# Gather and weight rings of a decoder layer: v ring 6 to 5 slots, query weight ring 4 to 5 and 6

## What is computed

```python
def peer_layer(x, w_q, sub_keys, u_table, v_table):
    q = (tok @ w_q).reshape(T, PEER_HEADS, 2, KEY_DIM)
    s = jnp.einsum('thcd,hckd->thck', q, sub_keys)
    s1, i1 = lax.top_k(s[:, :, 0], PEER_TOPK)
    s2, i2 = lax.top_k(s[:, :, 1], PEER_TOPK)
    cand = (s1[..., :, None] + s2[..., None, :]).reshape(T, PEER_HEADS, PEER_TOPK * PEER_TOPK)
    top, pos = lax.top_k(cand, PEER_TOPK)
    ...
    idx = e1 * N_KEYS + e2
    gates = jax.nn.softmax(top, axis=-1)
    ...
        u = u_table[ic]
        act = jax.nn.gelu(jnp.einsum('cd,chkd->chk', xc, u), approximate=False) * gc
        v = v_table[ic]
        return jnp.einsum('chk,chkd->cd', act, v)
```

## Time and profile before

| | |
|---|---|
| median of three runs | 3369.57 us (3368.59 to 3376.63) |
| profiled execution, its own time | 3396.82 us |
| its span | 3395.0 us |
| TensorE, matmuls | 2514.1 us busy, 74% of the span |
| VectorE | 2129.6 us, 63% |
| GpSimd | 2080.4 us, 61% |
| ScalarE | 859.2 us, 25% |
| DMA | 1209.32 MB, mean 356 GB/s |
| gathers of u and v | 1024 each, 1073.87 MB |
| granted clock of TensorE, mean | 0.843 |

### The profile page before, as it was taken

How to read it: one execution, slowest core, us unless ns; L and a number is a source line. 1 busy time by engine, 2 the same in 40 slices (tenths; PEclk the granted TensorE clock), 3 DMA queues, 4 the chain that set the end, 5 groups by cost and what they waited for, 6 DMA issues and landing times.

```text
span 3395.0 us, 33094 instructions
## 1 busy us (share of the span) xinstructions
PE 2514.1 (74%) x10304; PEld 1258.0 (37%) x10304; DVE 2129.6 (63%) x5664; ACT 859.2 (25%) x2635; POOL 2080.4 (61%) x2164
## 2 busy tenths in 40 slices
PE   8967888868888677767766677667976698765555
PEld 6754445534455233323333233322433243331111
DVE  2585556854669555884659646694658847586442
ACT  5334533125331132112211122112321133111111
POOL 0377566775667665665666656665666656666665
PEclk8989899988999787877898788887888878887777
DMA  9599899998999999998999989998899989999998
GB/s 306 175 338 379 324 363 398 399 373 304 363 394 377 398 374 341 406 380 305 345 379 397 365 301 344 395 393 329 322 371 405 377 294 331 383 405 350 381 369 318
DMA packets 383118, 1209.32 MB, mean 356 GB/s; under 512 B 43488, under 2 KB 84448, under 8 KB 382944
## 3 DMA queue, kind: packets, MB, share of 16 engines
q0 software_dynamic: 294912, 1073.87, 83.5%
q1 hardware_dynamic: 83616, 132.94, 11.0%
q10 hardware_dynamic: 4416, 0.40, 0.1%
HBM read 1199.20 MB, written 7.86 MB: 356 GB/s over the span
## 4 chain that ended last, share of the span: by engine, by line
PE 41%; issue 18%; DVE 12%; POOL 10%; DMA 7%; another core or an unknown queue 7%; ACT 4%; SPq 0%; DVEq 0%; ACTq 0%; POOLq 0%
PE psum L1014 19%; PE psum L843 5%; DVE big L1534 5%; POOL big L750 5%; POOL big L761 5%; DMA big<-in_peer_v,big 4%; PE psum L887 4%; PE psum L979 3%; PE psum L921 3%; PE psum L946 3%; DMA big<-in_peer_u,big 2%; PE psum L903 1%; DVE big L1347 1%; ACT big L1160 1%
## 5 line engine op out<-in xcount | busy, mean ns | idle before, releaser
L1014 PE MATMUL psum<-big 128*64 128x512 f32 x4096 | 1256.2, 743 | 550.7 <-issue 544.0
L761 POOL DMA_INDIRECT big<-in_peer_v,big x1024 | 1009.2, 986 | 718.1 <-PE psum L1014 311.8
L750 POOL DMA_INDIRECT big<-in_peer_u,big x1024 | 1025.8, 1002 | 443.8 <-issue 292.4
L1534 DVE CUSTOM_DVE_ANT_0 big<-big,psum 128x1024 f32<-128x1024 f32 x714 | 859.4, 1218 | 355.2 <-DMA big<-in_peer_u,big 283.1
L1014 PEld LDWEIGHTS psum<-big 128*64 128x64 f32 x4096 | 317.3, 161 | 1214.5 <-issue 1198.6
L1160 ACT ACTIVATE big<-big 128x64 f32<-128x64 f32 x1024 | 294.7, 339 | 863.5 <-PE psum L1014 400.9
L1534 DVE CUSTOM_DVE_ANT_0 big<-big 128x1024 f32<-128x1024 f32 x310 | 374.7, 1224 | 77.5 <-DMA big<-in_peer_u,big 72.2
L1347 DVE CUSTOM_DVE_ANT_0 big<-psum,big 128x512 f32<-128x512 f32 (+3 forms) x192 | 110.7, 577 | 425.4 <-PE psum L887 218.1
L979 PEld LDWEIGHTS psum<-big 128*128 128x128 f32 x2048 | 253.3, 201 | 94.1 <-issue 82.7
L979 PE MATMUL psum<-big 128*128 128x128 f32 x2048 | 272.4, 289 | 16.7 <-ACT big L1228 9.6
L887 PE MATMUL psum<-KT,big 64*128 64x512 f32 (+3 forms) x384 | 202.2, 613 | 79.6 <-issue 47.8
(11 more groups left out here) (141 smaller groups left out, 2137.2 us busy)
## 6 DMA issues: line engine op xcount, KB each, us to landing
big<-in_w_peer_q SPq DMA_DIRECT2D x108, 512.0 KB
big<-in_w_in SPq DMA_DIRECT2D x24, 1024.0 KB, 12.4
big<-in_peer_u,big POOLq DMA_INDIRECT x1024
big<-in_peer_v,big POOLq DMA_INDIRECT x1024
big<-in_w_out SPq DMA_DIRECT2D x2, 4096.0 KB, 22.7
big<-in_w_out SPq DMA_DIRECT2D x16, 512.0 KB
big<-in_w_in SPq DMA_DIRECT2D x28, 256.0 KB
V<-in_w_in SPq DMA_DIRECT2D x20, 256.0 KB
```

What stands on the lines that cost most here:

```text
L750: nc.gpsimd.indirect_dma_start(out=u_row(g), out_offset=None, in_=peer_u, in_offset=bass.IndirectOffsetOnAxis(ap=idx[:, t % 2, u_pick(p):u ...
L761: nc.gpsimd.indirect_dma_start(out=v_ring[:, g % RV, :], out_offset=None, in_=peer_v, in_offset=bass.IndirectOffsetOnAxis(ap=idx_v[:, t % ...
L1014: last = nc.tensor.matmul(pAcc[half_rows(c), n, :], sel[:, (g + c) % RD, :], v_ring[:, (g + c) % RV, n * COLS:(n + 1) * COLS], start=False ...
L1534: v.tensor_tensor_reduce(out=row_, in0=row_, in1=hn_ps if g >= MOVE_PICK else hn[:, hn_buf(t), :], scale=1.0, scalar=0.0, op0=ALU.mult, op ...
```

## The change

The v ring gets five slots instead of six, and the u ring keeps five to the end. The weight ring gets five, and from tile 3 on a sixth, in the half of `hn` that was the u ring's sixth. All 16 chunks of a tile are now used in reverse order in every other tile from tile 3 on (before, the four blocks were reversed and the four parts of a block stood in one order), so that the last five or six chunks of a tile can be the first of the next. Tile 3 keeps 5 chunks and tiles 4 to 7 keep 6, where 4 were kept. The slots are now given out by a list (`list_places`) that names for each load the one that it replaces.

```diff
-RU, RV = 5, 6
-WIDER_FROM = 61 * RU
-RW = 4
+RU, RV = 5, 5
+RW = 5
+WIDER_FROM = NARROW
...
+def query_part(t, n):
+
+    return divmod(4 * (PH // 2) - 1 - n if t >= EARLY and (t - EARLY) % 2 == 0 else n, 4)
...
+def ring_of(t):
+    return RW + 1 if t >= WIDER_FROM else RW
...
-    return t >= EARLY and i < RW
+    return t >= EARLY and i < ring_of(t - 1)
...
-                load_of[t, i] = load_of[t - 1, w_chunks(t - 1) - RW + i]
+                load_of[t, i] = load_of[t - 1, w_chunks(t - 1) - 1 - i]
...
+def list_places():
+
+    free, slot, before, widened = list(range(RW)), [], [], False
+    held = []
+    for m, (t, i) in enumerate(W_LOADS):
+        prev = None
+        if t >= WIDER_FROM and not widened:
+            widened, r = True, RW
+        elif free:
+            r = free.pop(0)
+        else:
+            prev = min(held, key=lambda o: W_ENDS[o])
+            held.remove(prev)
+            r = slot[prev]
+        slot.append(r)
+        before.append(prev)
+        held.append(m)
+    return slot, before
...
-                if m >= RW:
-                    te, ie = W_ENDS[m - RW]
+                if W_BEFORE[m] is not None:
+                    te, ie = W_ENDS[W_BEFORE[m]]
                     sp.wait_ge(w_used, w_first(te) + ie + 1)
+                elif m == W_WIDER:
+                    sp.wait_ge(y_stored.sem, y_stored.at(1, 1))
...
-                if u_before(g) is not None:
-                    pool.wait_ge(u_used.sem, u_before(g) + 1)
-                elif g >= RU:
-                    pool.wait_ge(y_stored.sem, y_stored.at(1, 1))
+                if g >= RU:
+                    pool.wait_ge(u_used.sem, g - RU + 1)
...
-                        last = nc.tensor.matmul(pT[:, j % 2, i * P:(i + 1) * P], w_ring[:, m % RW, k, i * P:(i + 1) * P],
-                                                turned[:, 2 * kp + k, :], start=(kp == 0 and i == 0 and k == 0),
+                        last = nc.tensor.matmul(pT[:, j % 2, i * P:(i + 1) * P], w[:, k, i * P:(i + 1) * P],
+                                                turned[:, 2 * part_ + k, :], start=(kp == 0 and i == 0 and k == 0),
```

More of the change, by code:

```diff
@@ L205, in w_place @@
     return lin(t, slot_of(t, 27 + 6 * (i // 4) + i % 4))
+def query_part(t, n):
+    return divmod(4 * (PH // 2) - 1 - n if t >= EARLY and (t - EARLY) % 2 == 0 else n, 4)
 def query_block(t, j):
-    return PH // 2 - 1 - j if t >= EARLY and (t - EARLY) % 2 == 0 else j
+    return query_part(t, 4 * j)[0]
+def ring_of(t):
+    return RW + 1 if t >= WIDER_FROM else RW
 def kept(t, i):
-    return t >= EARLY and i < RW
+    return t >= EARLY and i < ring_of(t - 1)
 def list_chunks():
@@ L233 @@
 W_LOADS, W_ENDS, W_LOAD_OF = list_chunks()
[L236 to L250, removed]
+def list_places():
[15 more added lines that the diff above has]
+    return slot, before
+W_SLOT, W_BEFORE = list_places()
+W_TURN = [W_SLOT[:m].count(r) for m, r in enumerate(W_SLOT)]
+W_WIDER = W_SLOT.index(RW)
 def hn_buf(t):
@@ L360, in hybrid_layer, with w_slot @@
         rms_x = w_out_flat[:, 8080:8088]
-        def u_row(g):
-            return hn[:, 1, :] if u_slot(g) == RU else u_ring[:, u_slot(g), :]
+        def w_slot(m):
+            return hn[:, 1, :] if W_SLOT[m] == RW else w_flat[:, W_SLOT[m]]
         key_raw = V[:, 3:5, :].rearrange("p t n -> p (t n)").rearrange("p (g n) -> p g n", g=2 * PH)
@@ L454, in hybrid_layer @@
         y_stored = signal("y_stored", 1, 16)
-        w_loaded = [sem(f"w_loaded{r}") for r in range(RW)]
-        u_loaded = [sem(f"u_loaded{r}") for r in range(RU + 1)]
+        w_loaded = [sem(f"w_loaded{r}") for r in range(RW + 1)]
+        u_loaded = [sem(f"u_loaded{r}") for r in range(RU)]
         v_loaded = [sem(f"v_loaded{r}") for r in range(RV)]
@@ L625, in load_w @@
                 t, i = W_LOADS[m]
-                if m >= RW:
-                    te, ie = W_ENDS[m - RW]
+                if W_BEFORE[m] is not None:
+                    te, ie = W_ENDS[W_BEFORE[m]]
                     sp.wait_ge(w_used, w_first(te) + ie + 1)
+                elif m == W_WIDER:
+                    sp.wait_ge(y_stored.sem, y_stored.at(1, 1))
                 if i < w_out_chunks(t):
-                    sp.dma_start(w_flat[:, m % RW], w_out[i * P:(i + 1) * P, :]).then_inc(w_loaded[m % RW], 16)
+                    sp.dma_start(w_slot(m), w_out[i * P:(i + 1) * P, :]).then_inc(w_loaded[W_SLOT[m]], 16)
                 else:
[L632 to L635, removed]
+                    block, kp = query_part(t, i - w_out_chunks(t))
+                    sp.dma_start(w_slot(m).rearrange("p (k n) -> p k n", k=2),
+                                 w_peer_q[2 * kp * P:2 * (kp + 1) * P, block * COLS:(block + 1) * COLS]
+                                 .rearrange("(k p) n -> p k n", p=P)).then_inc(w_loaded[W_SLOT[m]], 16)
             def store_q(u):
@@ L724, in _ @@
                     for m in range(RW, len(W_LOADS)):
-                        if w_place(*W_ENDS[m - RW]) == lin(e, s):
+                        place = lin(2, SLOTS - 4) if m == W_WIDER else w_place(*W_ENDS[W_BEFORE[m]])
+                        if place == lin(e, s):
                             load_w(m)
@@ L745, in gather_u @@
                     pool.wait_ge(idx_ready.sem, idx_ready.at(t, p // TOPK + 1))
-                if u_before(g) is not None:
-                    pool.wait_ge(u_used.sem, u_before(g) + 1)
-                elif g >= RU:
-                    pool.wait_ge(y_stored.sem, y_stored.at(1, 1))
+                if g >= RU:
+                    pool.wait_ge(u_used.sem, g - RU + 1)
                 nc.gpsimd.indirect_dma_start(
-                    out=u_row(g), out_offset=None, in_=peer_u,
+                    out=u_ring[:, g % RU, :], out_offset=None, in_=peer_u,
                     in_offset=bass.IndirectOffsetOnAxis(ap=idx[:, t % 2, u_pick(p):u_pick(p) + 1], axis=0))\
-                    .then_inc(u_loaded[u_slot(g)], 16)
+                    .then_inc(u_loaded[g % RU], 16)
             def gather_v(g):
@@ L942, in out_proj @@
                 if w_out_chunks(t):
-                    pe.wait_ge(w_loaded[m % RW], 16 * (m // RW + 1))
-                w = w_flat[:, m % RW] if w_out_chunks(t) else w_out_sb[:, k, :] if t else w_out_rows[:, k, :]
+                    pe.wait_ge(w_loaded[W_SLOT[m]], 16 * (W_TURN[m] + 1))
+                w = w_slot(m) if w_out_chunks(t) else w_out_sb[:, k, :] if t else w_out_rows[:, k, :]
                 for n in range(2):
@@ L1527, in dot_row @@
                 g = t * PICKS + p
-                dve.wait_ge(u_loaded[u_slot(g)], 16 * (u_turn(g) + 1))
+                dve.wait_ge(u_loaded[g % RU], 16 * (g // RU + 1))
                 if g == MOVE_PICK or p == 0 and t > IN_PSUM:
```

6 lines of the change are left out of this document (3 added, 3 removed).

## The result

| | us |
|---|---|
| before, median of 4 runs | 3370.76 (3368.59 to 3376.63) |
| after, median of 4 runs | 3411.39 (3401.69 to 3424.10) |
| ratio | 1.0098, 95% interval 1.0064 to 1.0131 |
| profiled execution of after: time, span | 3401.83, 3400.0 |

The change makes the kernel slower by 33 us by the ratio (22 to 44 by its interval), 41 by the medians.

The account below looks back on a forecast made before the run. No compute engine was full; the DMA engines were nearly so outside attention, and late gathers, held most by v slots, lost time. Terms -12 + 0 + 0 + 8 + 15 + 35 + 8 = +54 on 3369.6 gave 3424 us, range 3360 to 3500.

Parts of the forecast that it names:

- Fewer loads: Query stretches: 9 weight transfers of 512 KB go, 12 us gained, bounds 0 and 15.
- Weights deeper ahead: Query matmuls: they never wait for a weight transfer, so the fifth and sixth weight slots gain nothing more, 0 us.
- u ring back to five: From pick 305 on: no gain of the sixth u slot is seen in attention, so 0 us, bound 20.
- v ring: All v gathers: with five slots every second one needs its slot a whole pair later; +8, +15, +35 and +8 by stretches.
- Tail: Last 12 v pairs after the last u gather: a loop of two pairs, 4.0 us a pair, +8 us (6 to 16).
- Last stage: Gathers, dots and row sums only: some seven late releases plus the low clock, +15 us, bounds 0 and 27.
- Paced stretches: Between attention and query stretches: a third of the last stage's rate, +35 us, bounds 0 and 99.
- attention: Attention stretches: half a microsecond in some of about 30 bursts of pairs, +8 us, bounds 0 and 40.
- Query stretches: Where query weights load beside gathers: DMA engines stay full with fewer gathers queued, 0 us; below 400 GB/s, forecast too low.
- Bytes alone: Rival, whole kernel: five slots keep the DMA as full as six, only saved bytes count, 3356 us; chance 0.15.
- Even: Rival: the tail's 8 us and the bytes' 12 nearly cancel, -4 to +8, 3366 to 3378 us; chance 0.20.
- The v ring everywhere: Rival, every stretch: the odd gather's wait lengthens each pair, +100 to +190, 3470 to 3560 us; chance 0.15.

Follow-up runs that it names:

- its repetition: The changed kernel run once more, on one chip with its parts, against the kernel before: 3410.95 us, ratio 1.0090.
- experiment 2: The kernel before with the u ring at five slots to the end, v ring six, weights as before: 3379.16 us, ratio 0.9993.
- experiment 5: The kernel before with the last 24 v picks also using the five empty u slots, eleven in all: 3372.50 us, ratio 0.9980.
- experiment 8: The kernel before with u ring five, 4 weight loads fewer, and the last 24 v picks in eleven slots, on a faster chip: 3148.63 us, ratio 0.9982.
- experiment 1: The kernel before with only the v ring cut from six slots to five, all weight loads kept: 3419.68 us, ratio 1.0131.
- experiment 3: The changed kernel with v ring six and weight ring four, then five from tile 3; 4 loads fewer than before: 3370.12 us, ratio 0.9969.

## Why the prediction was right, point by point

Forecast +54 us, 3424; measured 3411, +33 by the ratio, and +30 and +41 in two other sets. The case that the forecast took (+10 to +100, the v ring outweighing the bytes) is the one that came. That the total lies so near is in part luck, as the points below tell: one term was ten times too large, and another was worked out from it.

By stretches, measured between the starts of fixed pairs of v rows (512 pairs, 0 to 511; of each 64 the query stretch is 43 to 60, attention 11 to 26, paced what lies between, in the table from pair 0 to 448; last stage 448 to 499, tail 499 to 511): (a) mean of after and its repetition, less the mean of before and of experiments 2 and 5; (b) the change on the faster chip less experiment 8 on such a chip, which has 4 of the 9 loads off and the longer ring in the tail.

| stretch | forecast | (a) | (b) |
|---|---|---|---|
| paced and attention | +35 +8 | +27 | +39 |
| query, with the 9 loads | -12 | -8 | -8 |
| last stage | +15 | +2 | +2 |
| tail | +8 | +7 | +14 |
| sum | +54 | +28 | +47 |

For the tail, (a) leaves experiment 5 out. Paced stretches and attention stand together since profiles of the same rings trade time between them: beside the rows of tiles 2 to 6 attention takes 489 to 519 us in the three with six v slots, and the paced stretches 931 to 962. Their sum is 1451 to 1460, and with five slots 1454 (experiment 1), 1467 and 1485. From pair 0 to 448 single profiles of the same rings lie up to 19 us apart, so the +27 and +39 are rough, and one profile with five slots stands inside the range of six.

- *Fewer loads, -12.* Right. 99 loads, 4.72 MB less. The query stretches beside the rows of tiles 2 to 6, which are the fronts of tiles 3 to 7 with the nine loads, take 508 to 509 us in the three profiles with loads taken away (after, its repetition, experiment 3) and 514 to 521 in the four without: 9.5 us less by the means, and 9 to 14 by the runs. What one load is worth isn't settled: four gave as much as nine in experiment 3, and nothing to be seen in section 8.
- *Weights deeper ahead, 0.* Right: no weight load is among what the query matmuls of after wait for, as before. Idle time ahead of L996, in us and times:

```profile
  issue: 102.4, 104
  ACT big L1245: 14.8, 12
```

- *u ring back to five, 0, bound 20.* Right: -2 us (-11 to +6). The reason given, that attention ran no better with six, was good enough; a sharper one that the stops suggest is that GpSimd, taking u and v in turn, stops at whichever ring is shorter. From 340 to 765 us, where both kernels have five u slots, it stopped 65.8 us at u and 10.3 at v; after stops 3.4 at u and 67.2 at v, as the waits of that stretch tell:

```profile
POOL big L777 <- PE psum L1031: 60.2, 30, 5.7
...
POOL big L777 <- remote: 7.0, 4, 2.3
POOL big L766 <- DVE big L1551: 3.4, 3, 1.7
```

- *v ring, +66 over all its terms.* Sign right, size half too large: +44 alone (33 to 55). The mechanism is the one drawn: the stops stand ahead of the odd gathers now, and the tail shows the loop of two pairs.
- *Tail, +8.* Right, +7.4 over three profiles with five slots and three with six (before, experiments 2 and 3); 3.93 us a pair for 4.0.
- *Last stage, +15.* Mis-sized, measured +1.5. The failed step is "With five slots it would have stopped at the odd gather of 3221.84 already, two issues earlier: 2 x 1.24 = 2.5 us of gathers lost", seven times, and the low clock on top. The stops in the stage went from 29.4 to 32.0 us and the gathers stayed 156, so the late releases hold the shorter ring hardly longer than the longer one. I had counted an earlier stop as lost transfers, and no row showed that the DMA engines had run dry by then. (The granted clock of 0.72 also means more than half of the time at the low level, 0.56 of it, and not "nearly half".) On the faster chip this stage runs at 409 GB/s with five slots and with six (windows below), with a DMA share of 1.03 both times, so there the transfers bound it, not the ring.
- *Paced stretches, +35, and attention, +8.* Together +27 and +39 for 43: the largest share is where the sum had put it. How it divides between the two isn't told by these profiles. The 35 was a third of the last stage's rate, and that rate was ten times too high (1.5 us for 15); the fraction was as wrong the other way. That their product came near is luck. I had argued that "much of a row's lateness lies under other work" of TensorE. It is the stretches with that other work that lose, and the last stage, where the pairs mostly follow evenly, that doesn't. That the unevenness is why, is my reading and was not tested by itself.
- *Query stretches, 0.* The window fell from 405 to 399 GB/s and seven slices with it, which was named as the sign of a forecast too low. The time in them tells otherwise: experiment 1, with all loads, has 520.5 us in tiles 2 to 6, inside the 514 to 521 of the three with six slots and all loads. No cost is seen.

The rule of the Trainium skill (Perfetto Trace Analysis, Optimization Strategy), that a repeated gap can mean too few buffers, had the sign: the stops at the v slot went from 443 to 586 us and the time up. It gives no size, and the length of the gaps gives none either: with six slots 443 us of them stood in the trace, and a seventh gained nothing beside five of u.

**The rivals.** *Bytes alone*: fell with experiment 1, +44 with all bytes in place; its -12 lies in what the profiles show. *Even*: fell; the intervals of all three comparisons begin above +20 us. *The v ring everywhere, +100 to +190*: fell for five slots; four bring more than that, +215. *Doesn't do what it says*: excluded by the 99 loads.

## What to carry to other kernels

Where one queue issues gathers for two rings in turn, the stops move from one ring to the other, so those at one ring don't tell what a slot of it is worth: judge a ring by taking one slot away and by adding one. A consumer that takes rows in pairs makes an odd ring behave like the next smaller even one for every second gather. Here the cost lay in the stretches in which TensorE has other work between the pairs, and not in the last stage. A ring that has emptied at the end of a phase (here u's, in the tail) is memory that costs nothing to lend.

## What was not expected of the hardware

The kernel before takes 3370 to 3382 us on some chips and 3153 us on others. What differs can be placed. Windows over the pairs 205 to 218 (attention), 218 to 233 (paced), 235 to 252 (query) and 459 to 498 (last stage), first experiment 8, then the change on the faster chip:

```profile
1494.00:1560.00 66.00, 54.95 (x245) 24.75 (x242) 42.25 (x98) 22.50 (x58) 49.76 (x54) 0.95 1.03 409
1560.00:1638.00 78.00, 60.51 (x249) 25.49 (x250) 53.87 (x110) 23.38 (x55) 57.86 (x61) 0.98 1.03 409
1650.00:1752.00 102.00, 70.76 (x340) 36.61 (x342) 81.20 (x241) 15.29 (x43) 62.93 (x67) 0.83 1.03 406
2904.00:3104.00 200.00, 118.32 (x312) 28.80 (x310) 98.39 (x175) 23.80 (x82) 146.90 (x157) 0.70 1.03 409
```

```profile
1507.00:1576.00 69.00, 57.20 (x250) 25.77 (x251) 41.73 (x99) 22.79 (x59) 49.95 (x54) 0.93 1.03 409
1576.00:1655.00 79.00, 64.57 (x253) 26.55 (x253) 55.59 (x113) 23.64 (x56) 58.42 (x63) 0.91 1.02 405
1665.00:1765.00 100.00, 71.23 (x336) 37.49 (x334) 80.69 (x235) 15.40 (x43) 63.55 (x67) 0.83 1.02 400
2940.00:3141.00 201.00, 105.31 (x312) 28.12 (x312) 98.55 (x177) 24.02 (x83) 146.14 (x156) 0.82 1.03 409
```

By the starts of the same pairs, attention takes 66 us in experiment 8 where it took 90 before, the paced stretch 78 for 91, the last stage 201 for 220, and the query stretch 101 for 103. So the highest rates are nearly the same on both, 405 to 409 GB/s; on the slower chip, of these four, the query stretch alone reaches them. The granted clock of TensorE differs too: the runs of the kernel before have 0.84 to 0.85 on the chips of the first two sets and 0.88 to 0.89 on the others. It doesn't explain the last stage, where 201 us were made at 0.70 and 220 at 0.72; for attention (0.95 against 0.79) no run tells cause from result. The Trainium skill (HBM Reference, Specifications) says that a core alone gets more than the share of some 358 GB/s; the 409 agree.

In the waits of GpSimd, the profiles from the slower chips have 64 to 95 stops at a v slot that the trace gives to no instruction (131.2 and 201.6 us in the two kernels), but only 4 with four v slots. In the kernel before, such a release comes 1.8 to 9.1 us after the recorded end of the pair that had to be done, 3.7 in the middle; one with a name can be late too, as that of 3228.18 in the earlier trace rows. On the faster chips there are none without a name, and in the change a stopped gather goes out 0.20 to 0.27 us after the end of the pair that it waited for. It has

```profile
POOL big L777 <- PE psum L1031: 392.7, 251, 8.4
...
POOL big L766 <- DVE big L1551: 60.2, 120, 2.4
```

I took these late releases for a part of the change's price. They are not needed for it: without them it is +41 us. What delays them on some chips, and whether they make the 220 us between the chips, was not settled; no run here varied it.
